# Weight products in passes within half a slot, the two output banks in turn

## What is computed

```python
def swiglu(h, w_gu, w_down):
    g, u = jnp.split(h @ w_gu, 2, axis=-1)
    return (jax.nn.silu(g) * u) @ w_down
# first block, per layer (lru_w_in and lru_w_o in the second layer):
proj = h @ w_in            # 2048 -> 1088
... out @ w_o              # 2048 -> 2048
h = h + swiglu(rms_norm(h, norm_ffn[layer]), ffn_w_gu[layer], ffn_w_down[layer])
# second block, per layer:
proj = jnp.einsum('bsd,dc->bsc', h, w_in[layer])    # 2048 -> 8200
x = x + jnp.einsum('bsc,cd->bsd', y, w_out[layer])
```

## Time and profile before

| | us |
|---|---|
| median of 3 runs (3193.36 to 3193.66) | 3193.53 |
| the profiled execution's own time | 3193.34 |
| its span, first to last instruction | 3191.6 |
| mean granted TensorE clock | 0.998 of full |

### The profile page before, as it was taken

One profiled execution on the slowest core, in us unless ns is written; L12 is line 12 of the kernel. 1 busy time (PEld: TensorE's weight loads), 2 busy tenths in 40 slices (PEclk: granted clock), 3 DMA queues, 4 the chain that ended last, 5 costly groups with the idle time before them and its releaser, 6 DMA issues.

```text
span 3191.6 us, 60705 instructions
## 1 busy us (share of the span) xinstructions
PE 3159.5 (99%) x26086; PEld 3125.1 (98%) x26086; DVE 1862.5 (58%) x2026; ACT 1604.3 (50%) x2077; POOL 0.2 (0%) x4
## 2 busy tenths in 40 slices
PE   8999999999999999999999999999999999999999
PEld 8999999999999999999999999999999999999999
DVE  6555555445555477765554555556667665666664
ACT  6554443334343466754443344446556655646663
POOL 0000000000000000000000000000000000000000
PEclk9999999999999999999999999999999999999999
DMA  6335555645556455555565555655656555655654
GB/s 219 116 113 165 175 179 171 199 156 171 171 175 196 155 176 184 168 185 186 190 212 177 171 184 188 207 158 154 179 159 173 171 159 174 175 167 165 174 155 141
DMA packets 525217, 550.00 MB, mean 172 GB/s; under 512 B 10640, under 2 KB 518800, under 8 KB 523920
## 3 DMA queue, kind: packets, MB, share of 16 engines
q1 hardware_dynamic: 525072, 547.88, 55.0%
HBM read 541.56 MB, written 2.10 MB: 170 GB/s over the span
## 4 chain that ended last, share of the span: by engine, by line
PE 96%; DVE 2%; ACT 2%; issue 0%; DMA 0%; SPq 0%; DVEq 0%; ACTq 0%
PE ps L593 87%; PE ps L660 2%; PE ps L1020 1%; PE ps L919 1%; PE ps L910 0%; PE ps L730 0%; PE ps L927 0%; PE ps L891 0%; DVE w_lo L1536 0%; PE ps L836 0%; DMA raw<-mla_w_in_dram 0%; PE ps L758 0%; DVE w_lo L1540 0%; ACT w_hi L1046 0%; PE ps L886 0%
## 5 line engine op out<-in xcount | busy, mean ns | idle before, releaser
L593 PE MATMUL ps<-x_hi,w_hi 128*128 128x256 f32 (+1 forms) x5840 | 1654.0, 283 | 23.3 <-DVE w_lo L1669 10.4
L593 PE MATMUL ps<-x_lo,w_hi 128*128 128x256 f32 (+1 forms) x5840 | 1653.1, 283 | 0.0
L593 PE MATMUL ps<-x_hi,w_lo 128*128 128x256 f32 (+1 forms) x5840 | 1648.6, 282 | 0.0
L593 PEld LDWEIGHTS ps<-x_hi,w_hi 128*128 128x128 f32 x5840 | 1101.7, 189 | 31.1 <-issue 17.5
L593 PEld LDWEIGHTS ps<-x_lo,w_hi 128*128 128x128 f32 x5840 | 1099.5, 188 | 0.8
L593 PEld LDWEIGHTS ps<-x_hi,w_lo 128*128 128x128 f32 x5840 | 1100.0, 188 | 0.0
L1540 DVE TENSOR_TENSOR w_lo<-raw,w_hi 128x1024 fp32r<-128x1024 f32 (+3 forms) x496 | 651.1, 1314 | 580.4 <-ACT w_hi L1051 580.0
L1051 ACT ACTIVATE w_hi<-raw 128x1024 fp32r<-128x1024 f32 (+3 forms) x496 | 559.9, 1130 | 723.9 <-PE ps L593 704.6
L1536 DVE TENSOR_TENSOR w_lo<-raw,w_hi 128x1024 fp32r<-128x1024 f32 (+2 forms) x496 | 595.4, 1202 | 512.9 <-ACT w_hi L1046 508.5
L1046 ACT ACTIVATE w_hi<-raw 128x1024 fp32r<-128x1024 f32 (+2 forms) x496 | 513.5, 1037 | 401.1 <-PE ps L593 398.7
L593 PE MATMUL ps<-hid_hi,w_lo 128*128 128x272 f32 (+1 forms) x1408 | 401.0, 285 | 0.0
(11 more groups left out here) (289 smaller groups left out, 2316.2 us busy)
## 6 DMA issues: line engine op xcount, KB each, us to landing
raw<-ffn_w_gu_dram SPq DMA_DIRECT2D x176, 1024.0 KB, 5.1
raw<-w_in_dram SPq DMA_DIRECT2D x128, 1024.0 KB, 5.4
raw<-ffn_w_down_dram SPq DMA_DIRECT2D x64, 1408.0 KB, 6.4
raw<-w_out_dram SPq DMA_DIRECT2D x32, 1024.0 KB, 5.3
raw<-lru_w_in_dram SPq DMA_DIRECT2D x24, 1024.0 KB, 5.5
raw<-mla_w_o_dram SPq DMA_DIRECT2D x16, 1024.0 KB, 5.2
raw<-lru_w_o_dram SPq DMA_DIRECT2D x16, 1024.0 KB, 5.2
raw<-lru_y_gates_dram SPq DMA_DIRECT2D x8, 1280.0 KB, 5.6
```

What stands on the lines that cost most here:

```text
L593: mm = pe.matmul(out, l, r, start=first and k == 0 and i == 0, stop=last and k == kn - 1 and i == 2)
```

## The change

`use_slot` goes through each half of a slot in steps. Without a callback the steps are pass by pass: all chunks of the half with `w_hi` and `x_hi`, then all with `w_hi` and `x_lo`, then all with `w_lo` and `x_hi`; PE waits for ACT's half (`hi_half`, `hi_made`) before the first pass and for DVE's (`lo_half`, `lo_made`) before the third. With a callback the three parts of a chunk stay together, and the waits are as before. In both cases the innermost loop is now over the two banks, so that neighbouring matmuls write to different banks and stream the same moving tile (in slots with `moving_weights` the same part of the weights).

```diff
--- before.py
+++ after.py
@@ -576,19 +576,25 @@
 
                 hi, lo = slot_view(w_hi, n % 2, kn, width), slot_view(w_lo, n % 2, kn, width)
                 half = 4 if kn == 11 else kn // 2
-                for k in range(kn):
-                    if k == 0:
-                        pe.wait_ge(lo_half, n + 1 + 4 * rn)
-                    if k == half:
+                for part, ks in enumerate((range(half), range(half, kn))):
+                    if part == 1:
                         mm.then_inc(slot_half, 1)
-                        pe.wait_ge(lo_made, n + 1 + 4 * rn)
                     if at_chunk is not None:
-                        at_chunk(k0 + k)
-                    x_of = (a_hi[:, k0 + k, :], a_lo[:, k0 + k, :])
-                    if ahead is not None and k0 + k < 4:
-                        x_of = (ahead[:, 0, k, :], ahead[:, 1, k, :])
-                    for out, c in outs:
-                        for i, (w, x) in enumerate(((hi, x_of[0]), (hi, x_of[1]), (lo, x_of[0]))):
+                        pe.wait_ge((lo_half, lo_made)[part], n + 1 + 4 * rn)
+                        steps = [(k, i) for k in ks for i in range(3)]
+                    else:
+                        pe.wait_ge((hi_half, hi_made)[part], n + 1 + 4 * rn)
+                        steps = [(k, i) for i in range(3) for k in ks]
+                    for k, i in steps:
+                        if at_chunk is not None and i == 0:
+                            at_chunk(k0 + k)
+                        if at_chunk is None and i == 2 and k == ks[0]:
+                            pe.wait_ge((lo_half, lo_made)[part], n + 1 + 4 * rn)
+                        xs = (a_hi[:, k0 + k, :], a_lo[:, k0 + k, :])
+                        if ahead is not None and k0 + k < 4:
+                            xs = (ahead[:, 0, k, :], ahead[:, 1, k, :])
+                        w, x = ((hi, xs[0]), (hi, xs[1]), (lo, xs[0]))[i]
+                        for out, c in outs:
                             l, r = (x[:, c], w[:, k, :]) if moving_weights else (w[:, k, c], x)
                             mm = pe.matmul(out, l, r, start=first and k == 0 and i == 0,
                                            stop=last and k == kn - 1 and i == 2)
```

## The result

The changed kernel takes 3218.12 us (median of 4 runs, 3217.43 to 3218.78), the kernel before beside it 3193.55 (4 runs, 3193.36 to 3193.66). The ratio is 1.0077, with a 95% interval of 1.006 to 1.0094: slower by 24.6 us, where 15.8 us less was forecast, and above the range too.

What follows compares the result with a forecast made beforehand. PE, busy for 99% of the span, was taken as the bound through its interval between matmuls. Gains of 10.9 us (order), 4.0 (down stage) and 0.9 (wait), together 15.8 off 3193.5, gave 3177.7 us, range 3164 to 3207.

Steps and rivals of the forecast that it cites:

- Nothing added, met waits free: Slots of `use_slot`: same matmuls on the same tiles, same release places; new waits, already met, cost nothing.
- The wait at slot 3: Slot 3 of the first turn: low parts needed 16 matmuls later, so PE's wait for `w_lo` goes, 0.9 us gained.
- The order of the tiles: Line 593, 256 columns: chunk changed after two matmuls takes 115.94 ns, not 116.94; 10,896 matmuls, 10.9 us gained; chance 0.46.
- rows 8: Forget-gate product, lines 955 and 956: 32 matmuls at 115.9 ns, stationary tiles of 8 or 16 columns; taken as the new rate.
- "no change" at 272 columns: 272-token stages: interval stays at 125.0 ns under the new order, bounds plus or minus 0.2 ns.
- rows 9: Lines 660, 593 and 836 at 272 columns: four orders within 0.2 ns of each other, so bank and chunk changes cost nothing.
- The down stage falls: FFN down stage, 256 tokens: 1,848 matmuls go from 118.12 to 115.94 ns, 4.0 us gained.
- Alternation of banks costs nothing: Line 593: changing bank each matmul costs nothing, bounds 0.4 ns either way; rival that it saves, 3169.6 us, chance 0.04.
- The clock: PE's granted clock stays as before; rival that it falls to 1.2 GHz in spells, 3207 us at ten, chance 0.01.
- the no-change rival: 256-column stages: rate ignores the order and 116.94 ns stays; 3190.4 us, chance 0.27.
- the new stationary tile: Line 593, 256 columns: a new stationary tile at each matmul costs, 118.12 ns, 12.9 us added; 3205.5 us, chance 0.22.

Runs made afterwards that it cites:

- the four kernels with the old waits that are shown first: Changed kernel with old waits: chunk order kept with banks in turn, 3192.83 us; passes one bank at a time, 3197.79; one bank per half, 3214.0; its own order, 3217.96.
- the last kernel of this study: Kernel before with 256-token activations' chunks 256 elements apart, and the second FFN's hidden state moved to starts 24 and 56: 3162.84 us, ratio 0.9902.
- the first packed kernel: Kernel before, order and waits untouched, 256-token activations' chunks 256 elements apart in place of 272, from the LRU's output product on: 3165.01 us, ratio 0.9918.
- the first experiment: Changed kernel with old waits and a chunk's three parts kept together, each going to both banks in turn: 3192.83 us, ratio 0.9998.

## Why the prediction was wrong

1. *Nothing added, met waits free*: right. The change's order with the old waits takes the same time.

2. *The wait at slot 3*: the number came by luck. The 0.95 us between starts there are gone, and at 100 us the changed kernel is 0.9 us ahead of the one before by the start of the same matmul. But the hole is also gone in the four kernels with the old waits that are shown first, and in the last kernel of this study, whose code up to there is that of the kernel before; in the first packed kernel, with the same code again, it is 0.62 us. What differs from run to run is when ACT begins that half: 28.29 us in the profiled run before, 27.06 after. The kernels with the old waits spread over 1.2 us among themselves at 100 us. That the moved wait wins anything is not shown.

3. *The order of the tiles*: this step failed. "For 256 columns I take the 115.9 of rows 8" should have been 119.17, 2.23 ns above the old interval in place of 1.0 below it. The prediction named what it hung on ("the narrow stationary tiles there may be what saves the nanosecond"), and the series with 16 stationary columns bears that out: the change's order takes 116.7 with them and 119.1 with 128. A row with another stationary width was no row for this. The "no change" at 272 columns was 0.83 ns off, four times its bound: rows 9 had not a chunk change after two matmuls among their orders.
   The sum with what was measured: 10,896 x 2.23 = 24.3 us, and the 272-token stages another 5.1, so 29.4; the measured 24.6 is less, and the missing part lies in the second block. Of the 10,896, 4,128 are in FFN 1 and 672 in the recurrent layer's output product, and these lost 2.2 ns each. The 6,096 of the second block would have lost 13.6 us and lost 7.7: its slots did not stand at 116.94 before (most long pieces lay at 117.5 to 118.1, and at 118.3 to 120.2 after). Why was not followed further.

4. *The down stage falls*: wrong, it stayed. Taking turns was no difference: `x_hi` and `x_lo` take turns in the same way in the up stage. `hid_hi` and `hid_lo` stand at another place in memory than `x_hi`, and the series with the real tensors and the same order gives the 118.2 from that alone.

5. *Alternation of banks costs nothing*: right, shown by the first experiment and by the series.

6. *The clock*: right for the whole, 0.999 of full, and 1.00 in the long stages. The short stretches at 0.50 are there in both kernels, at other places: 1317 us before and 1348 after, and at the start of the second block 6.7 us before and 3.3 after. The "TensorE: Matmul & The Clock Gate" page of the Trainium skill, section "A second HAM failure mode: psum-queue depth-cycling", tells of a loss in a kernel that cycles through banks and idles between its groups of matmuls; here the bank changes with each matmul, PE is busy throughout, and the trace shows no loss from it.

The formula quoted under the no-change rival, from the section "Back-to-back issue gap" of the same page of the Trainium skill, is given there for an isolated matmul; for a stream of loads and matmuls the section says that both set the spacing.

The forecast's direction came out wrong though the slower side was among the rivals at 3205.5. That rival named the wrong cause, the new stationary tile: the first experiment changes it with every matmul and is not slower. Nor did any rival hold that the place of the tiles in memory sets the rate. The row that should have raised the question was there: 118.12 in the down stage against 116.94 in the up stage, with the same tile shapes and the same order, differs in the tensors (and in 11 chunks in place of 8).

What is shown: the loss is in PE alone, it comes from the order of moving tiles whose starts differ modulo 64 elements, it is absent where all starts agree, and the distance of moving to stationary start then sets the interval, up to the choice of gait. That the read of the next stationary tile and that of the moving tile get in each other's way is the nearest reading of this (the narrow stationary tile and the shifted one speak for it), but it was only argued. The "TensorE: Matmul & The Clock Gate" page of the Trainium skill, section "Step-by-step: what each phase is for", says that loading the next tile's weights takes no read bandwidth from the running matmul. Here a shift of the stationary tile by 16 elements changed the interval from 120.0 to 113.3 ns, so for these operands the load's place is not indifferent to the running matmul; whether by read bandwidth, no run shows. Open are the rule for a cycling start, and what chooses between 113.3 and 117.8.

## What to carry to other kernels

Where PE is busy for 99% and its interval lies above the columns' own time, put the matmuls of one stage into a series of their own, with the real tiles in their real places, before any rewriting of the order: a single run gave the FFN intervals of every order of this study to a tenth of a nanosecond. Choose the distance between chunks so that all moving tiles start at one place modulo 64 elements, and try that place against the stationary tile's, since a bad one (120.0 ns at a distance of 0) is worse than no common place at all (116.94); it won 0.8 to 1.0% here, where none of the four new orders won anything. A rate taken from another row is good only for the same tile shapes, stationary width included, and the same tensors.

## What the hardware showed that I had not expected

With 128 stationary columns in this format a steady series never came under 111.6 ns a matmul, at 128, 192, 208 or 232 moving columns; 512 columns took 226.7 to 233.4. Series of 256 columns took anything from 113.3 to 120.9 ns, and a displacement of 4 elements of `hid_hi` (24 to 28) was worth 6.6 ns. Such a value is steady within a series, but the same series took 113.3 or 117.8 by what ran before it, and in the kernels the same product changed between these two at a stop of 1.3 or 2.0 us, in either direction.
